# Preparing the queries, keys and values of a latent attention: rope by exchanged weight columns and one table, norms read from the PSUM banks

## What is computed

```python
def _mla(h, w_down, q_norm, w_uq, kv_norm, w_ukv, w_o):
    down = h @ w_down                                    # 1024 -> 256 + 128 + 32
    c_q = _rmsnorm(down[..., :256]) * q_norm
    c_kv = _rmsnorm(down[..., 256:384]) * kv_norm
    k_rope = down[..., 384:]                             # 32, shared by the heads
    q = (c_q @ w_uq).reshape(B, S, 16, 64 + 32)
    kv = (c_kv @ w_ukv).reshape(B, S, 16, 64 + 64)
    k_nope, v = kv[..., :64], kv[..., 64:]
    q_nope = q[..., :64]
    q_rope = _apply_rope(q[..., 64:], cos, sin)
    k_rope = _apply_rope(k_rope, cos, sin)
    s = (q_nope . k_nope + q_rope . k_rope) * 96 ** -0.5 # per head
    return (softmax(s) @ v).reshape(B, S, 1024) @ w_o

def _apply_rope(x, cos, sin):                            # pairs of neighbours
    x1, x2 = x[..., 0::2], x[..., 1::2]
    return stack([x1 * cos - x2 * sin, x1 * sin + x2 * cos])
```

## Time and profile before

| | us |
|---|---|
| median of 3 runs (lowest, highest) | 1806.93 (1803.66, 1807.07) |
| the profiled execution | 1807.55 |
| its span | 1805.8 |
| down products to the first score | 1092.27 to 1162.38 |
| attention of the latent heads, to the first product of `project` | 1162.38 to 1217.47 |

### The profile page before, as it was taken

How to read it: one execution, slowest core, us unless ns; L and a number is a source line. 1 busy time by engine, 2 the same in 40 slices (tenths; PEclk the granted TensorE clock), 3 DMA queues, 4 the chain that set the end, 5 groups by cost and what they waited for, 6 DMA issues and landing times.

```text
span 1805.8 us, 26569 instructions
## 1 busy us (share of the span) xinstructions
PE 1640.8 (91%) x11088; PEld 1463.5 (81%) x11088; DVE 1256.6 (70%) x1475; ACT 872.3 (48%) x1014; POOL 156.5 (9%) x165
## 2 busy tenths in 40 slices
PE   6999989538699998998999997889999999999997
PEld 6999879428589997975899985458989989989996
DVE  5777759565567777545677762455887987987886
ACT  4333445321244344343443342345777667767775
POOL 1000013304000000025000002450000000000000
PEclk9999999759699998999999998998999999999998
DMA  8777523010068774430577751003999988889983
GB/s 309 278 272 273 213 94 141 1 70 1 24 269 307 282 302 174 167 114 22 229 279 271 266 210 47 0 1 109 376 335 329 342 326 327 336 326 331 339 326 127
DMA packets 51786, 385.71 MB, mean 214 GB/s; under 512 B 5872, under 2 KB 6208, under 8 KB 7760
## 3 DMA queue, kind: packets, MB, share of 16 engines
q1 hardware_dynamic: 50400, 376.16, 56.6%
q0 software_dynamic: 1264, 7.82, 1.1%
HBM read 382.90 MB, written 1.05 MB: 213 GB/s over the span
## 4 chain that ended last, share of the span: by engine, by line
PE 77%; DVE 11%; ACT 5%; issue 4%; POOL 2%; DMA 1%; DVEq 0%; ACTq 0%; SPq 0%
PE bank L297 20%; PE bank L299 20%; PE bank L298 20%; PE bank L1148 5%; PE bank L457 2%; ACT sb_whi L265 2%; DVE sb_wlo L269 1%; PE bank L1676 1%; PE bank L1635 1%; PE bank L1850 1%; PE bank L611 1%; DVE sb_wlo L2106 1%; PE bank L1791 1%; DVE sb_p L1137 1%; ACT sb_whi L2100 1%
## 5 line engine op out<-in xcount | busy, mean ns | idle before, releaser
L269 DVE TENSOR_TENSOR sb_wlo<-sb_raw,sb_whi 128x2048 fp32r<-128x2048 f32 x137 | 313.8, 2291 | 204.7 <-ACT sb_whi L265 204.6
L297 PE MATMUL bank<-sb_xhi,sb_whi 128*128 128x256 f32 x1360 | 388.6, 286 | 15.7 <-POOL sb_qd L1109 8.4
L298 PE MATMUL bank<-sb_xlo,sb_whi 128*128 128x256 f32 x1360 | 386.4, 284 | 0.0
L299 PE MATMUL bank<-sb_xhi,sb_wlo 128*128 128x256 f32 x1360 | 386.3, 284 | 0.0
L265 ACT ACTIVATE sb_whi<-sb_raw 128x2048 fp32r<-128x2048 f32 x137 | 261.4, 1908 | 191.2 <-PE bank L299 185.3
L297 PEld LDWEIGHTS bank<-sb_xhi,sb_whi 128*128 128x128 f32 x1360 | 262.6, 193 | 19.8 <-issue 9.3
L298 PEld LDWEIGHTS bank<-sb_xlo,sb_whi 128*128 128x128 f32 x1360 | 262.6, 193 | 1.1
L299 PEld LDWEIGHTS bank<-sb_xhi,sb_wlo 128*128 128x128 f32 x1360 | 262.5, 193 | 0.0
L297 PE MATMUL bank<-sb_whi,sb_slots_hi 128*128 128x256 f32 x896 | 257.8, 288 | 0.0
L299 PE MATMUL bank<-sb_whi,sb_slots_lo 128*128 128x256 f32 x896 | 252.6, 282 | 0.0
L298 PE MATMUL bank<-sb_wlo,sb_slots_hi 128*128 128x256 f32 x896 | 251.7, 281 | 0.0
(11 more groups left out here) (466 smaller groups left out, 2640.2 us busy)
## 6 DMA issues: line engine op xcount, KB each, us to landing
sb_raw<-in_ffn SPq DMA_DIRECT2D x98, 1024.0 KB, 4.9
sb_raw<-in_moe SPq DMA_DIRECT2D x86, 1024.0 KB, 5.5
sb_ada_raw<-in_ada SPq DMA_DIRECT2D x32, 1536.0 KB, 6.9
sb_cst<-in_moe SPq DMA_DIRECT2D x28, 1024.0 KB, 5.4
sb_xn<-in_moe SPq DMA_DIRECT2D x27, 1024.0 KB, 5.5
sb_ada_raw<-in_moe SPq DMA_DIRECT2D x27, 1024.0 KB, 5.7
sb_raw<-in_w_in SPq DMA_DIRECT2D x13, 1024.0 KB, 4.9
sb_raw<-in_na_qk SPq DMA_DIRECT2D x8, 1024.0 KB, 5.0
```

Of the source, the lines that this page charges most:

```text
L269: e.tensor_tensor(wlo[s][:, :], raw[s][:, :], whi[s][:, :], ALU.subtract).then_inc(s_lo[s], 1)
L297: e.matmul(dst, wh, xh, start=first, stop=False, skip_group_check=skip)
L298: e.matmul(dst, wh, xl, start=False, stop=False, skip_group_check=skip)
L299: return e.matmul(dst, wl, xh, start=False, stop=last, skip_group_check=skip)
```

## The change

The query weights are laid out differently on the host. Each head had 96 columns (64 plain, 32 rope); now it has 128: after them come its 32 rope columns again, with the two of each pair exchanged. One table `turned` holds ones for the 64 plain rows, the cosine for the next 32 and the signed sine for the last 32. A head's scores are a sum over all 128 rows, so cosine part and sine part need not be added to one another before: the key holds its finished rope rows twice, at 64 to 95 and at 96 to 127.

So per round the product with `turn`, ACT's copy of the queries, POOL's and DVE's multiplications and DVE's addition are gone, and one DVE multiplication of the bank with the table stands for them. Squares are taken from the banks, as are the scaled latents; the copies to `lat` are gone, as are the zeroing by POOL and both meetings. The sum of squares of the queries is taken ahead of the rope columns of the down product. Two rounds of queries stand ahead of the values, which have four banks. `wuq` has its own buffer and is loaded early; the tables (1024 columns) and `wukv` go into `ada_raw` after the last modulation unit of `ffn3`. `attend` takes its waits from a function of the head.

```diff
+    cos, sin, both = (np.ones((P, T)) for _ in range(3))
+    swap = np.arange(ROPE) ^ 1
+    sign = np.where(np.arange(ROPE) % 2 == 0, -1.0, 1.0)
...
+    both[HD:QH], both[QH:] = cos[HD:QH], sign[:, None] * sin[QH:]
...
+    attn |= {"turned": both, "cos": cos, "sin": sin, "place": place, "placeturn": placeturn}
...
             m = pe.step(lambda e, q=q: e.matmul(bk[:, q * T:(q + 1) * T], *scores(i, q), start=mask is None, stop=True),
-                        *m_ready, m_sread.get(i - 2))
+                        *m_ready(i), m_sread.get(i - 2))
...
             gd = dma(pool, wd[:, :, :], a["mla_down"], "down", *marks)
-            got = [dma(pool, tab[:, :], a["att"], "tab"), dma(pool, wukv[:, :], a["mla_ukv"], "ukv"),
-                   dma(pool, wuq, a["mla_uq"], "uq", (env["s_ada"], ADA_UNITS), m_in[-1])]
...
+            got_q = dma(pool, wuq[:, :, :], a["mla_uq"], "uq")
+            got_tab = dma(pool, tab, a["att"][:, tab0:tab0 + D], "tab", (env["s_ada"], ADA_UNITS))
+            got_kv = dma(pool, wukv, a["mla_ukv"], "ukv")
...
-            m1 = act.step(lambda e: e.activation(lat[:, 0:2, :], bank[4][:, :].rearrange("p (k t) -> p k t", k=2),
-                                                 ACT.Copy), m)
-            m2 = act.step(lambda e: e.activation(lat[:, 2, :], bank[5][:, 0:T], ACT.Copy), m)
-            m3 = dve.step(lambda e: e.tensor_copy(kr[0:ROPE, :], bank[6][0:ROPE, 0:T]), m)
-            meet()
...
+            down(bank[4][:, 0:T], 0, P)
+            m_q = down(bank[4][:, T:2 * T], P, P)
+            m_kv = down(bank[5][:, 0:T], 2 * P, P)
+            ms_q = square_sum(lambda k_: bank[4][:, k_ * T:(k_ + 1) * T], 2, bank[3][:, 0:T], m_q)
+            m_kr = down(bank[6][0:ROPE, 0:T], 3 * P, ROPE)
+        mr = inv_root(rstd[:, 0, :], bank[3][:, 0:T], 1.0 / QL, EPS, ms_q)
...
+        ms = square_sum(lambda k_: bank[5][:, 0:T], 1, bank[7][:, 0:T], m_kv, ms_q)
+        m_krc = dve.step(lambda e: e.tensor_copy(kr[0:ROPE, :], bank[6][0:ROPE, 0:T]), m_kr, m_cq)
...
-        m_pad = [pool.step(lambda e, z=z: e.memset(z[QH:P, :, :], 0.0)) for z in (q, k)]
...
-        for i in range(AH // 2):
-            kb, qb, tb = bank[0 + i % 2], bank[2 + i % 2], bank[4 + i % 2]
...
-            m = pe.step(lambda e, qs=qs, tb=tb: e.matmul(tb[0:QH, :], A("turn", QH), qs,
-                                                         start=True, stop=True), mq_[i], mt_.get(i - 2))
...
-        meet()
...
+        def queries(i):
+            qb = bank[2 + i % 2]
...
+                    m = pe.step(lambda e, hh=hh, j=j, kt=kt: e.matmul(
+                        qb[:, j * T:(j + 1) * T], wuq[:, kt, hh * P:(hh + 1) * P], lat[:, kt, :],
+                        start=kt == 0, stop=kt == 1), got_q, m_cq, m_qs.get(i - 2))
+            m_qs[i] = dve.step(lambda e: e.tensor_tensor(
+                q[:, 2 * i:2 * i + 2, :], qb[:, :].rearrange("p (h t) -> p h t", h=2),
+                A("turned").rearrange("p (n t) -> p n t", n=1).broadcast_to([P, 2, T]), ALU.mult), m)
+
+        def keys(i):
...
+            m_krs[i] = pool.step(lambda e: e.tensor_copy(
+                k[rp, 2 * i:2 * i + 2, :], kr[rp, :].rearrange("p (n t) -> p n t", n=1).broadcast_to([HD, 2, T])), m_krot)
+
+        queries(0)
+        queries(1)
+        for b in range(NB):
+            for hf in range(2):
+                bk = bank[4 + 2 * b + hf]
+                m = pe.step(lambda e, b=b, hf=hf, bk=bk: e.matmul(
+                    bk[:, :], lat[:, 2, b * P:(b + 1) * P], vcols[:, 8 * hf:8 * hf + 8, HD:2 * HD],
+                    start=True, stop=True), got_kv, m_ckv, m_krot)
...
+        for i in range(AH // 2):
+            keys(i)
+            if i > 1:
+                queries(i)
+        dve.wait(m_krs[AH // 2 - 1])
+        pool.wait(m_krs[AH // 2 - 1])
...
+                   lambda i: [m_ks[AH // 2 - 2 + i % 2], m_qs[i // 2], m_krs[i // 2], m_v], follow)
...
+def turned_columns(w):
+
+    w = w.reshape(QL, AH, QH)
+    return np.concatenate([w, w[:, :, HD + (np.arange(ROPE) ^ 1)]], axis=2).reshape(QL, AH * P)
```

More of the change, by code:

```diff
@@ L1769, in latent, with A @@
         marks = env["scratch_free"][0]
+        spare = env["spare"]
         lat = sb("lat", [P, 3, T], ctx=ctx)
-        kr = sb("kr", [P, T], ctx=ctx)
-        tab = sb("tab", [P, sum(n for _, n in att.values())], ctx=ctx)
-        wukv = sb("wukv", [P, AH * 2 * HD], ctx=ctx)
+        kr = rstd[:, 0, :]
         v = sb("mla_v", [P, NB, D], ctx=ctx)
-        wuq = env["ada_raw"][:, :, :].rearrange("p k n -> p (k n)").rearrange("p (k n) -> p k n", k=2)
-        def A(name, n=None, p0=0, p1=P):
+        wuq = sb("wuq", [P, 2, AH * P], ctx=ctx)
+        wukv, tab, tab0 = spare[:, 0:2 * D], spare[:, 2 * D:3 * D], att["turned"][0]
+        def A(name, p0=0, p1=P):
             at, w = att[name]
-            return tab[p0:p1, at:at + (n or w)]
-        rp = slice(HD, QH)
+            return tab[p0:p1, at - tab0:at - tab0 + w]
+        rp = slice(HD, P)
         with ExitStack() as c1:
@@ L1818, in latent @@
[L1818 to L1838, removed]
-        for i in range(AH // 2):
-            kb, qb, tb = bank[0 + i % 2], bank[2 + i % 2], bank[4 + i % 2]
[L1841 to L1846, removed]
+        for l in (act, dve, pool):
+            l.wait(m_kr)
@@ new lines, in latent @@
+        m = None
+        for i, name in enumerate(("place", "placeturn")):
+            m = pe.step(lambda e, i=i, name=name: e.matmul(bank[6][:, i * T:(i + 1) * T], A(name, 0, ROPE), kr[0:ROPE, :],
+                                                           start=True, stop=True), got_tab, m_krc)
+        m1 = dve.step(lambda e: e.tensor_tensor(kr[rp, :], bank[6][rp, 0:T], A("cos", HD), ALU.mult), m, got_tab)
+        m2 = dve.step(lambda e: e.tensor_tensor(k[rp, 0, :], bank[6][rp, T:2 * T], A("sin", HD), ALU.mult), m)
@@ new lines, in queries @@
+            m_qs[i] = dve.step(lambda e: e.tensor_tensor(
+                q[:, 2 * i:2 * i + 2, :], qb[:, :].rearrange("p (h t) -> p h t", h=2),
+                A("turned").rearrange("p (n t) -> p n t", n=1).broadcast_to([P, 2, T]), ALU.mult), m)
+        def keys(i):
+            kb = bank[i % 2]
+            for j in range(2):
+                m = pe.step(lambda e, j=j: e.matmul(kb[0:HD, j * T:(j + 1) * T], vcols[:, 2 * i + j, 0:HD], lat[:, 2, :],
+                                                    start=True, stop=True), m_ckv, m_ks.get(i - 2))
+            m_ks[i] = act.step(lambda e: e.activation(
+                k[0:HD, 2 * i:2 * i + 2, :], kb[0:HD, :].rearrange("p (h t) -> p h t", h=2), ACT.Copy), m)
+            m_krs[i] = pool.step(lambda e: e.tensor_copy(
+                k[rp, 2 * i:2 * i + 2, :], kr[rp, :].rearrange("p (n t) -> p n t", n=1).broadcast_to([HD, 2, T])), m_krot)
```

70 lines of the change are left out of this document (23 added, 47 removed).

## The result

| | before | changed |
|---|---|---|
| median, us (lowest, highest) | 1805.86 (1803.66, 1807.07), 4 runs | 1771.29 (1770.41, 1775.87), 4 runs |
| ratio | | 0.9819, interval 0.9803 to 0.9835 |
| profiled execution, span | 1805.8 | 1770.1 |
| down products to first score | 70.1 | 43.1 |

The new order of the preparation took what the sum said to within 0.2 us. What the sum missed is the length of the old preparation in other executions, and what lies around the stretch.

The account below looks back on a forecast made before the run. PE's queue plus its waits from first down product to first score (70.1 us) was taken as the bound. 1807.55 - 27.2 (preparation) - 1.3 (first exponential) = 1779.1, with the median 0.6 lower: 1778.5 us, range 1774 to 1785.

Parts of the forecast that it names:

- the sum: Piece lengths from first down product (1092.27) to first score, at 1135.2 instead of 1162.38: 27.2 us gained, 26.4 to 27.9.
- What bounds the kernel: PE's queue plus its waits, from first down product at 1092.27 to first score at 1162.38: 70.1 us.
- Placing: Placing the rope key after the rope columns: 4 PE records, 0.9 us taken from 0.9 to 2.1, to 1108.8.
- The narrowest place: First value product at 1112.3 finds scaled latent and rope key done at 1112.1, 0.2 us to spare.
- 1162.38: Time of the first score in the profiled execution before; the change was to bring it to 1135.2.
- the clock only as a rival: New preparation: one low stretch in dense work costs 3.4 us, 1782 (chance 0.12); half clock throughout, 1817 (0.04).
- The starting time: The profiled execution's 1807.55 us, from which gains were subtracted; the median of the runs was put 0.6 lower.
- The first exponential: At the attention's start, exponential's table load no longer waits for DVE: 1.3 us less, bounds 0 to 1.3.
- The table load counted single: Hiding the load before the first exponential gives 1.3 us; rival that it weighs double: 2.6, 1777.2, chance 0.04.
- Loads: Reordered `wuq`, tables and `wukv` cost 0; `wukv` lands near 1072, needed at 1107.8, 36 us of cover.
- no new wait: Rival: values wait for scaled latent and rope key on DVE, start at 1115 instead of 1112.3; 1781, chance 0.08.
- no gain given back: Rival: downstream, transfers at fixed times set the expert stage and the gain is lost; 1807, chance 0.03.

Follow-up runs that it names:

- idle products: Changed kernel with 8 additional products whose result nobody reads ahead of the transposes of the latent layer's two norms: 1770.08 us, 0.9812.
- the two with rows early: Changed kernel, gate-row product issued behind its head's scores: 1778.29 us; the same with 8 unread products ahead of the transposes of all norms but the first: 1777.04 us.
- the fed kernel: Kernel before with 13 products of 256 columns, results unread, laid into the three holes that the norms leave on PE: 1800.57 us, 0.9978.
- the four old executions: Three profiles of the kernel before and one of it with only the new order of loads (1805.65 us, 0.9999): first down product to first score 70.1, 74.2, 72.3, 74.1 us.

## Why the prediction missed, step by step

- **What bounds the kernel, and the sum over the preparation.** Right: forecast 42.9 us from the first down product to the first score (1135.2 less 1092.27), measured 43.1 in all six profiles that have it unchanged (three of the changed kernel, idle products, and the two with rows early). Placing 1.06 (0.9 taken, 0.9 to 2.1 given), values 3.60 (3.5 to 4.0), rounds 2.94. The narrowest place held, with 0.15 us to spare where the sum had 0.2.
- **"1162.38" and the 27.2 us are one execution's, and its stretch was the cheapest of four.** This is the step that failed. The old stretch entered the sum with its 70.1 us. It varies from 70.1 to 74.2 with the low clock behind the holes of the norms, and the mean of 72.7 gives a gain of 29.6 for the new order, not 27.2. The fed kernel puts 3.7 us of that mean on the clock. I had named the clock only as a rival for the new kernel. That the old kernel pays for it was in sight in the earlier trace rows (3.73 against 2.00 for two equal products) and the sum counted it; that it pays more in other executions was not, and the range had nothing for it.
- **The starting time: the same fault.** The sum began at the profiled execution's 1807.55 and went down by the 0.6 to the median of three runs, 1806.93. The later medians of before are 1805.14 (21 runs), 1805.11 (14) and 1805.22 (9). About 1.8 of the 7.2 us between 1778.5 and 1771.3 are this.
- **The first exponential: mis-sized.** 1.3 forecast; 1.47 in the first profiles, and 2.0 against the mean of before (3.53, 4.47, 4.46, 3.89), because low clock sat on its first scores too; the fed kernel, with PEclk 1.00 there, has 3.53. From first score to router the four old executions have 86.7 to 87.0 us and the first two changed ones 84.2 and 84.0 (the third 85.3, with 6.8 us of low clock in it): 2.4 us in the mean of three. The table load counted single: hiding it gave 1.47, not the 2.66 of load and drain that the Trainium skill ("ScalarE: Activation LUTs", What ACT_TABLE_LOAD costs) sets down.
- **The remainder.** Mean spans are 1803.4 (three profiles of before) and 1769.3 (three of the changed kernel): 34.1 us, of which preparation 29.1 (these three of before have 72.2 in the mean) and first score to router 2.4. The last 2.6 us lie in the start (0.7) and from the router on (1.9), where the forecast had 0 and where the executions of one kernel differ by more than that (8.4 us in the start of the down products of before, 4.0 from the router on in the changed kernel). The runs do not show a cause there.
- **Loads** cost 0, as forecast. **DVE** kept up, 0.69 on 128 partitions. **The range** was too narrow below: it had the run-to-run spread of the total, but not the spread of the stretch that the change replaced.
- **Rivals.** None of them came: no low clock in the new preparation, no new wait, no gain given back. The chance for faster (0.92) was right in sign; all rivals but one lay above the forecast, and the time came out below it.

## What to carry to other kernels

When a change closes holes on TensorE, the old stretch must be priced from several executions, or at the full clock plus a range for the low one: the same code took 70 to 74 us, and the denser one 43.1 each time. Ask of each product how soon its operand is made: moving one sum and two rounds of other products into the wait, and letting the contraction add what two engines had added before, freed some 25 us at equal clock with no faster instruction. Low clock costs where TensorE has its input; behind a norm that feeds it in halves, keeping the clock up took 0.2 us off one execution of the transposes and 1.1 to 1.7 off others, too little to show in the time of whole runs.

## What the runs showed of the hardware that I had not expected

One and the same hole of 4.5 us, with PE busy for 1.1 us in it, was followed once by 6.8 us of low clock, once by 13.7 and once by 17.1, and PE was busy for most of that time (9.07 of 11.70 us at 0.54). And a single wait of 3.57 us for a rope key cost the products behind it 2.6 us (values 6.20 instead of 3.60).
